# Turning the memory tokens with VectorE's 32x32 block transposes, and the layer norm's tail on pairs of tiles, in a one-core decoder trunk

## What is computed

```python
def rms_norm(x, g):
    xf = x.astype(jnp.float32)
    y = xf * lax.rsqrt(jnp.mean(xf * xf, axis=-1, keepdims=True) + EPS)
    return (y * g.astype(jnp.float32)).astype(x.dtype)

# once, for both layers
mkv = (rms_norm(mem, mem_norm_g) @ w_mem_kv).reshape(bsz, mlen, 2, MEM_HEADS, MEM_HEAD_DIM)
mem_k = rms_norm(mkv[:, :, 0], mem_k_norm_g)
mem_v = mkv[:, :, 1]

# even layer, convolution group: c is the depthwise convolution over 1024 channels
c = layer_norm(c, ln_g, ln_b)
o_b = (jax.nn.silu(c.astype(f32)) * jax.nn.silu(z_b.astype(f32))).astype(h.dtype)
```

## Time and profile before

| | us |
|---|---|
| median of 3 runs (1311.61 to 1311.96) | 1311.9 |
| the profiled execution | 1310.86 |
| its span | 1309.1 |
| TensorE busy | 1303.0 (100%) |
| VectorE busy | 988.7 (76%) |
| ScalarE busy | 749.9 (57%) |
| GpSimd busy | 90.4 (7%) |
| SyncE queue's bytes | 267.00 MB, 67.0% of 16 engines' time |

### The profile page before, as it was taken

The page is one execution under the profiler, slowest core; times in us unless marked ns, Lnnn a source line. Parts: engine busy times, 40 slices in busy tenths (PEclk is TensorE's granted clock), DMA queues, the critical chain, the costliest instruction groups (busy, mean ns, idle before and its releaser), DMA issues.

```text
span 1309.1 us, 17285 instructions
## 1 busy us (share of the span) xinstructions
PE 1303.0 (100%) x6221; PEld 1092.9 (83%) x6221; DVE 988.7 (76%) x1548; ACT 749.9 (57%) x1175; POOL 90.4 (7%) x91
## 2 busy tenths in 40 slices
PE   9999999999999999999999999999999999999998
PEld 9898888888888888888888888888888888888887
DVE  5467588888988898887667487797788788668563
ACT  6556643567435556586346447748657568554341
POOL 2000200102000100100000020020100200000000
PEclk9999999999999999999999999999999999999999
DMA  9675465876775996785768664765765766977662
GB/s 316 203 207 180 151 200 163 221 213 202 213 212 165 299 314 219 220 241 159 215 207 259 195 194 152 248 194 174 228 194 174 227 192 192 284 214 220 199 194 80
DMA packets 182158, 272.82 MB, mean 208 GB/s; under 512 B 42384, under 2 KB 63801, under 8 KB 182073
## 3 DMA queue, kind: packets, MB, share of 16 engines
q1 hardware_dynamic: 179353, 267.00, 67.0%
q10 hardware_dynamic: 2720, 4.72, 1.1%
HBM read 251.10 MB, written 20.58 MB: 208 GB/s over the span
## 4 chain that ended last, share of the span: by engine, by line
PE 98%; DMA 1%; DVE 0%; ACT 0%; issue 0%; SPq 0%; ACTq 0%
PE job L1990 58%; PE job L2000 29%; PE job L1987 2%; PE mixer L2212 1%; PE mixer L2200 1%; PE mixer L2011 1%; PE job L1997 1%; PE mixer L2122 1%; PE mixer L2222 1%; PE mixer L2230 1%; PE mixer L2102 1%; PE mixer L2135 1%; DMA raw<-in_ev_w_in_dram 1%; DVE wlo L1463 0%; PE mixer L2221 0%; PE mixer L2232 0%
## 5 line engine op out<-in xcount | busy, mean ns | idle before, releaser
L1990 PE MATMUL job<-whi,xhi 128*128 128x512 f32 x1660 | 660.6, 398 | 0.0
L1990 PE MATMUL job<-whi,xlo 128*128 128x512 f32 x1660 | 647.1, 390 | 0.0
L1463 DVE TENSOR_TENSOR wlo<-raw,whi 128x1024 fp32r<-128x1024 f32 x431 | 527.3, 1244 | 88.2 <-ACT whi L1094 87.2
L1094 ACT ACTIVATE whi<-raw 128x1024 fp32r<-128x1024 f32 x431 | 445.6, 1056 | 220.6 <-PE job L2000 180.8
L2000 PE MATMUL job<-wlo,xhi 128*128 128x512 f32 x1660 | 444.1, 389 | 0.0
L2000 PEld LDWEIGHTS job<-wlo,xhi 128*128 128x128 f32 x1660 | 311.6, 188 | 65.6
L1990 PEld LDWEIGHTS job<-whi,xhi 128*128 128x128 f32 x1660 | 311.9, 188 | 62.5
L1990 PEld LDWEIGHTS job<-whi,xlo 128*128 128x128 f32 x1660 | 312.0, 188 | 62.2
L1736 DVE SCALAR_TENSOR_TENSOR cvr<-cvr,vt 128x255 f32<-128x255 f32 (+14 forms) x240 | 99.2, 472 | 0.0
L1127 ACT ACTIVATE proj<-job,rstd 128x512 f32<-128x512 f32 x76 | 47.9, 683 | 64.4 <-PE job L2000 43.7
L1496 DVE TENSOR_TENSOR hid<-hid,job 128x512 f32<-128x512 f32 x46 | 29.5, 684 | 39.6 <-PE job L2000 39.6
(11 more groups left out here) (307 smaller groups left out, 957.0 us busy)
## 6 DMA issues: line engine op xcount, KB each, us to landing
raw<-in_od_w_in_dram SPq DMA_DIRECT2D x160, 512.0 KB, 4.1
raw<-in_ev_w_in_dram SPq DMA_DIRECT2D x143, 512.0 KB, 4.5
raw<-in_ev_w_out_dram SPq DMA_DIRECT2D x48, 512.0 KB, 5.3
raw<-in_od_w_out_dram SPq DMA_DIRECT2D x48, 512.0 KB, 5.5
raw<-in_w_mem_kv_dram SPq DMA_DIRECT2D x32, 512.0 KB, 4.9
proj<-turned_blocks SPq DMA_DIRECT2D x68, 128.0 KB, 5.2
turned_blocks<-proj SPq DMA_DIRECT2D x9, 512.0 KB, 4.4
turned_blocks<-mix SPq DMA_DIRECT2D x7, 512.0 KB, 3.7
```

What stands on the lines that cost most here:

```text
L1094: act(whi[:, c % RING, :, :], raw[:, c % RAWS, :, :], ACT.Copy).then_inc(s_hi, 1)
L1463: vec.tensor_tensor(wlo[:, c % RING, :, :], raw[:, c % RAWS, :, :], whi[:, c % RING, :, :].bitcast(F32), ALU.subtract).then_inc(s_lo, 1)
L1990: mm(pj[j % 2][n][:, :], x[:, s, cols], h, start=first, stop=False)
```

## The change

`mem` is loaded in another layout: partition 32b + j of `memx` holds, for a = 0 to 7, columns 512b to 512b + 511 of token 32a + j. A transpose of 32x32 blocks on VectorE (`do_mt`, eight steps of 128x512, two fills each) then gives tiles whose rows are features 512b + 32k + j', in `memt`, tiles 4 to 7 of `mix`. The rows of `w_mem_kv` and of `mem_norm_g` are loaded in the same order: each chunk of the memory jobs by four DMAs of 32 partitions, the gains in runs of 32 elements. ScalarE and VectorE split the fills from `memt`; TensorE's transposes are gone. ScalarE's squares become eight of 512 columns, whose sums stand by (b, j) in `msum`; GpSimd puts them by token into `mquar` in 16 copies, and VectorE adds the four quarters. The layer norm's tail works on pairs of tiles: VectorE multiplies by the token factors alone, and ScalarE applies gain and bias in one instruction per tile. Fills 40 to 47 move one position later, and a tap pair's planned share is 0.29 for 0.31. The last wait of the turn `lt` 7 is now for all 16 memory fills.

```diff
-CONV_SHARE = 0.31
+CONV_SHARE = 0.29
...
-                "d5e": .1, "d6": .25, "gate": .25, "za": .45, "glu": .45, "zg": .65, "lt": .47, "nt": .5, "xt": .18, "mf": .16, "bas": .1}
+                "d5e": .1, "d6": .25, "gate": .25, "za": .45, "glu": .45, "zg": .65, "lt": .47, "nt": .5, "xt": .18, "mt": .26, "mf": .16, "bas": .1}
...
-        stream(5, CH0[J_OB] + k // 2 - 3, [(("mf", F_OB + k), 0)])
+        stream(5, CH0[J_OB] + k // 2 - 2, [(("mf", F_OB + k), 0)])
...
-        stream(5, CH0[J_MEM] - 11 + k, [(("xt", F_MEM + k), 0)])
-        stream(5, CH0[J_MEM] - 2 + k, [(("xt", F_MEM + 8 + k), 0)])
+        for half, start in ((0, CH0[J_MEM] - 11 + k), (8, CH0[J_MEM] - 2 + k)):
+            if k % 2 == 0:
+                stream(5, start - 1, [(("mt", (half + k) // 2), 0)])
+            stream(5, start, [(("xt", F_MEM + half + k), 0)])
...
-    for n in range(10):
-        p = stream(2, p, [(("ln" + "abo"[i], n - i), 0) for i in range(3) if 0 <= n - i < 8] + [("wait", 1)])
+    for n in range(6):
+        p = stream(2, p, [(("ln" + "abo"[i], n - i), 0) for i in range(3) if 0 <= n - i < 4] + [("wait", 1 + n % 2)])
...
-        memx = reg[:, :].rearrange("p (t d) -> p t d", t=T)
+        memx = reg[:, :].rearrange("p (a d) -> p a d", a=8)
+        memt = mflat[:, 4 * S:8 * S].rearrange("p (k s) -> p k s", k=4)
...
+                if name == "mem":
+                    for b in range(4):
+                        src = w[name][:, c0:c0 + 512].rearrange("(b k j) n -> b j k n", b=4, j=32)[b, :, 2 * (c - CH0[j]):2 * (c - CH0[j]) + 2]
+                        sp.dma_start(raw[32 * b:32 * b + 32, c % RAWS, :, :], src).then_inc(s_raw[c % RAWS], 16)
+                    return
...
+            for n, (dst, src) in enumerate(vecs(vrow)[1:]):
+                if n == 0:
+                    src = src.rearrange("k p -> (k p)").rearrange("(b k j) -> k b j", b=4, j=32)
+                    dst = dst.rearrange("k (b j) -> k b j", b=4)
...
             def do_rstd(src):
+                if src == 1:
+                    gp.wait_ge(s_ss, 2)
+                    for a in range(4):
+                        for b in range(4):
+                            ins = nc.gpsimd.tensor_copy(mquar[32 * a:32 * a + 32, :, b], msum[32 * b:32 * b + 32, a:8:4])
+                    ins.then_inc(s_mquar, 1)
...
+                if F_MEM <= n < F_OB:
+                    sc.wait_ge(s_jt, turn_count["mt", (n - F_MEM) // 2])
+                    fill_wait(n)
+                    act(xhi[:, SLOT[n], :], memt[:, n % 4, :], ACT.Copy, scale=xt_gain(n)).then_inc(s_xh, 1)
+                    return
...
+                if src == 1:
+                    for a in range(8):
+                        ins = act(pflat[:, 512 * (a % 4):512 * (a % 4) + 512], memx[:, a, :], ACT.Square, accum_out=msum[:, a:a + 1])
+                        if a == 3:
+                            link(ins)
+                    ins.then_inc(s_ss, 1)
+                    return
...
-            def do_lnb(ct):
-                sc.wait_ge(s_xn, ct + 2)
-                act(cvr[:, ct, :], cvr[:, ct, :], ACT.Identity, bias=gain("ev_ln_b", ct)).then_inc(s_ly, 1)
-                sc.wait_ge(s_ly, ct + 1)
-                if ct >= 2:
-                    sc.wait_ge(s_mixb, ct - 1)
-                act(cvr[:, 8 + ct % 2, :], cvr[:, ct, :], ACT.Tanh, scale=0.5).then_inc(s_lt, 1)
+            def do_lnb(a):
+                sc.wait_ge(s_xn, a + 2)
+                for ct in (2 * a, 2 * a + 1):
+                    ins = act(cvr[:, ct, :], cvr[:, ct, :], ACT.Identity, bias=gain("ev_ln_b", ct), scale=gain("ev_ln_g", ct))
+                link(ins)
+                if a:
+                    sc.wait_ge(s_mixb, 2 * a)
+                act(cvr[:, 8:10, :], cvr[:, 2 * a:2 * a + 2, :], ACT.Tanh, scale=0.5).then_inc(s_lt, 1)
...
-                sc.dma_start(memx[:, :, 512 * b:512 * b + 512],
-                             mem[:, 512 * b:512 * b + 512].rearrange("(t p) d -> p t d", p=128)).then_inc(s_min, 16)
+                sc.dma_start(memx[32 * b:32 * b + 32], mem[:, 512 * b:512 * b + 512].rearrange("(a j) d -> j a d", j=32)
+                             ).then_inc(s_min, 16)
...
+            def do_mt(p):
+                ve.wait_ge(s_min, 64)
+                ve.wait_ge(s_xl, F_OA + 8 if p < 2 else F_MEM + 2 * p - 2)
+                vec.transpose(memt[:, 2 * (p % 2):2 * (p % 2) + 2, :].rearrange("p k s -> p (k s)"),
+                              memx.rearrange("p a (k j) -> p k a j", j=32)[:, 2 * p:2 * p + 2]).then_inc(s_jt, 1)
...
+                if src == 1:
+                    ve.wait_ge(s_mquar, 1)
+                    link(vec.tensor_reduce(ssq[:, src, :], mquar[:, :, :], AX.X, ALU.add))
...
+            def do_lna(a):
                 ve.wait_ge(s_xn, 1)
+                v = cvr[:, 2 * a:2 * a + 2, :]
+                vec.tensor_tensor(v, v, lnacc[:, :].unsqueeze(1).broadcast_to([128, 2, S]), ALU.mult).then_inc(s_xn, 1)
+
+            def do_lno(a):
+                c = cvr[:, 2 * a:2 * a + 2, :]
+                ve.wait_ge(s_lt, a + 1)
+                ve.wait_ge(s_z, 2 * a + 2)
+                link(vec.scalar_tensor_tensor(out=c, in0=cvr[:, 8:10, :], scalar=1.0, in1=c, op0=ALU.add, op1=ALU.mult))
+                v = mix[:, 8 + 2 * a:10 + 2 * a, :]
+                vec.scalar_tensor_tensor(out=v, in0=c, scalar=0.25, in1=v, op0=ALU.mult, op1=ALU.mult).then_inc(s_mixb, 2)
...
-                    ve.wait_ge(*((s_z, 16) if e == 6 else (s_xl, F_OA + 8)))
+                    ve.wait_ge(*((s_z, 16) if e == 6 else (s_xl, F_OB)))
...
             def do_xt(n):
-                if F_H <= n < F_H + 12:
+                if F_MEM <= n < F_H + 12:
                     return
...
-                elif n < F_OB:
-                    src, k = memx, n - F_MEM
-                    pe.wait_ge(s_min, 64)
```

More of the change, by code:

```diff
@@ L403, in prog @@
         qgain = sb("qgain", [128, 1])
+        msum = sb("msum", [128, 8])
+        mquar = sb("mquar", [128, T, 4])
         rows = sb("rows", [128, 2, 128], F32R)
@@ L497, in prog @@
         turn_no = {i: n for n, i in enumerate(i for st, i in plan if st == "lt")}
-        turn_count = {q: n + 1 for n, q in enumerate(q for q in plan if q[0] in ("lt", "nt"))}
+        turn_count = {q: n + 1 for n, q in enumerate(q for q in plan if q[0] in ("lt", "nt", "mt"))}
         def exchanged(e, transfers=5):
@@ L644, in prog @@
         s_xn = sem("ln_reciprocals_then_scaled")
-        s_ly = sem("ln_affine")
+        s_mquar = sem("mem_square_sums_by_token")
         s_lt = sem("ln_tanh")
@@ L699, in banks @@
             if step == "xt":
-                return [] if F_H <= i < F_H + 12 else [i % 3 if 8 <= i < F_OB else i % 4]
+                return [] if F_MEM <= i < F_H + 12 else [i % 3 if 8 <= i < F_OA else i % 4]
             if step == "mao":
@@ L789, in turned @@
         def turned(n):
-            return n + 1 if n < F_OA else n - F_MEM + 17 if n < F_OB else n - F_H - 12 + 33
+            return n + 1 if n < F_OA else n - F_H - 12 + 17
         def mix_tile(n):
@@ L1088, in split @@
                     return
-                sc.wait_ge(s_raw[c % RAWS], 16 * (c // RAWS + 1))
+                sc.wait_ge(s_raw[c % RAWS], 16 * (c // RAWS + 1 + 3 * sum(CH0[J_MEM] <= b < CH0[J_MEM + 4] for b in range(c % RAWS, c + 1, RAWS))))
                 if c >= RING:
@@ L1161, in do_rstd @@
                     sc.wait_ge(s_xl, F_H + 8)
+                if src == 1:
[5 more added lines that the diff above has]
+                    return
                 o = 2048 if src == 0 else 0
-                link(act(pflat[:, 0:2048], (memx if src == 1 else hid)[:, 0, :], ACT.Square, accum_out=ssq[:, src, 0:1]))
-                ins = act(pflat[:, o:o + 2048], (memx if src == 1 else hid)[:, 1, :], ACT.Square, accum_out=ssq[:, src, 1:2])
+                link(act(pflat[:, 0:2048], hid[:, 0, :], ACT.Square, accum_out=ssq[:, src, 0:1]))
+                ins = act(pflat[:, o:o + 2048], hid[:, 1, :], ACT.Square, accum_out=ssq[:, src, 1:2])
                 ins.then_inc(s_ss, 1)
@@ L1352, in squares @@
                 if i == 4:
-                    sc.wait_ge(s_xp, turned(F_MEM + KT - 1))
+                    sc.wait_ge(s_xl, F_OB)
                 unused = reg[:, 3072:4096] if i >= 4 else scr
@@ L1505, in do_first @@
                 ve.wait_ge(s_vt, 1)
+            def do_mt(p):
[3 more added lines that the diff above has]
+                              memx.rearrange("p a (k j) -> p k a j", j=32)[:, 2 * p:2 * p + 2]).then_inc(s_jt, 1)
             def do_xt(n):
                 ve.wait_ge(s_xh, n + 1)
+                if F_MEM <= n < F_OB:
+                    vec.scalar_tensor_tensor(out=xlo[:, SLOT[n], :], in0=memt[:, n % 4, :], scalar=xt_gain(n),
+                                             in1=xhi[:, SLOT[n], :].bitcast(F32), op0=ALU.mult, op1=ALU.subtract).then_inc(s_xl, 1)
+                    return
                 if F_H <= n < F_H + 12:
@@ L1756, in do_lnr @@
```

(6 more changed lines are left out.)

1 line of the change is left out of this document (removed).

## The result

The changed kernel takes **1313.47 us** at the median of 20 runs (1312.44 to 1314.57), the kernel before 1311.46 us at the median of 20 beside it (1311.05 to 1311.96). The ratio is 1.0016, with a 95% interval of 1.001 to 1.0023. It is slightly slower, where 1307.9 us was forecast. Its profiled execution took 1313.76 us, 2.90 more than the profiled execution of before, with a span of 1312.0.

A forecast was written before the change was run, and what follows sets the result against it. TensorE, busy 1303.0 of 1309.1 us, was taken as the bound. Removing 16 transpose pairs at 0.253 us saves 4.05 us, all else hidden: 1311.9 - 4.05 = 1307.9 us, 8-in-10 range 1307.2 to 1310.4.

The forecast's parts named there:

- Layer norm: VectorE's layer norm tail: 24 instructions of 256 become 12 of 512, some 2 us less, off the path; ScalarE about even.
- cost to TensorE nothing: Conv taps packed closer by the smaller share: at worst 3.0 us unplanned VectorE work; thinnest lead 3.4 us, at chunk 108.
- the cover is the lead of the chunk remainders: Chunks 150 to 190: VectorE's remainders at least 8.1 us ahead of TensorE, which was to hide the added work.
- rival 1: VectorE waits for GpSimd's copies, using up the lead; TensorE stands 2 to 4 us; 1310 to 1312 us; 12%.
- VectorE, turns and remainders: Memory stretch: eight turns add 5.6 us, fill remainders from SBUF save 1.0; lead expected to stay near 8 us.
- rival 2: Small losses together: remainders 1.4 to 4 us late around chunks 160 to 175; 1309.5 to 1312 us; 10%.
- Square sums: ScalarE's squares 6.5 us against 4.2; GpSimd's 16 copies 0.15 us each, 2.4 in all; VectorE waits about nothing, at most 9.3.
- The transposes: TensorE's 16 pairs of memory transposes in as many chunk slots: 0.253 us a pair, 4.05 us gained by removing them.
- SyncE: Memory chunk loads as four DMAs: 1.7 us of issue a chunk, under 2.72; any 1.3 us wait covered by the lead.
- rival 3: SyncE's queue becomes the bound in chunks 160 to 191; slower by 0.2% from 0.87 us an issue, up to 1366 us; 4%.
- The conv half's fills: Fills before chunk 192, one slot later: 8.1 us of margin leaves over 3 us, so no cost.
- The sign that I named: A TensorE wait on remainders near chunk 166 would prove the forecast wrong by rival 1.

The follow-up runs named there:

- the pair of 1311.9 and 1307.85: Changed kernel, memory fills 34 to 39 up to three positions earlier, lnm at 172: 1311.9 us; with the last two additions moved to VectorE too: 1307.85 us.
- the version with all four edits: Changed kernel with memory fills earlier, lnm at 172, square sums' factors at 164 and the last two additions on VectorE: 1307.48 us, ratio 0.997.
- the last version: Changed kernel with memory fills earlier, lnm at 172 and the last two additions on VectorE, factors not moved: 1307.85 us (1307.0 to 1311.39).

## Why the prediction was wrong

**The step that failed** is "*Layer norm* ... off the path" together with "cost to TensorE nothing" for the taps, and with them the sentence that the cover is the lead of the chunk remainders. The sum has no term for GpSimd's additions or for where their products stand in the plan. That lead is one margin of several. The first use of the layer norm on TensorE is `lnm`, which had 0.3 us of margin, not 8; and the 3925 ns of the earlier trace rows, which I quoted for rival 1, were the first of the two additions that it waits for. I used that row as a price for copies and did not ask who waited for the additions themselves. Nor did I work out the plan's new positions: the smaller share and the new steps moved `lnm` one chunk forward, 2.72 us, against those 0.3. It measured 2.73 us of wait and 1.8 of lower clock, 4.5 in the profiled execution. Wait and fill stall alone, 2.7 and 1.4 us, eat the gain of 4.05; the clock's 1.8, with the first chunks and chunk 93, make the profiled execution slower. The run of the kernel before with `lnm` at 170 and its twin with two additions on VectorE (1312.83 and 1311.48 us) show this without the change; the pair of 1311.9 and 1307.85 shows it in the changed kernel.

**"VectorE, turns and remainders ... Net 4.6 us in 48 us, hidden by the lead"** failed in its cover, not in its price. A turn took 0.70 us as said; a remainder from SBUF 0.48 and not 0.42, so 5.6 and not 4.6 us were added. For chunk remainders the cover held, though the lead did not stay near 8: its lowest value between chunks 150 and 190 sank from 8.2 to 5.3 us (chunks 156 and 157). A fill's remainder is made only 1.2 chunks before its use, and fill 39 had 3.3 us. TensorE's own gain is what eats such a margin: it arrives up to 4 us earlier at everything that it did not have to wait for before. It cost 1.37 us. This is rival 2 in its place (chunk 167) and its size (1.4 us), for the most part; that rival had 10%.

**"Square sums ... it stands still for about nothing"**: the copies took 246 ns each on the mean (4.55 us for 16, median 182 ns, one 1092), where I took 150, and VectorE waited 1.72 us. ScalarE's eight squares ended 5.1 us after they began, where I had 6.5. Rival 1 in its own form, the lead of the remainders used up, did not come; with the wait moved away the kernel took 0.65 us less, which is not resolved.

**What was right.** The transposes: 0.25 us a pair and 4.05 us in all, to the hundredth. That gain showed at the end only where nothing else was late: 1311.43 - 1307.48 = 3.95 us in the version with all four edits, 0.4 us from the forecast. SyncE: four DMAs for one cost nothing (1311.2 against 1311.22), rival 3 falls; in the changed kernel a piece took 0.427 us to issue at the median and landed in 4.1, where a whole load of the memory had landed in 4.9. (Rival 3's threshold for a time slower by 0.2% was mis-worked: with its own 12 us of lead it is 0.83 us an issue and not 0.87.) The conv half's fills, one slot later, brought no wait. The taps' closer packing costs nothing by itself (1311.32 against 1311.29), but it also moves what stands behind it, which the prediction left out. The advice against a transpose on VectorE did not matter: VectorE was at 75%, TensorE at 99%.

**The sign that I named** as proof against me, a TensorE wait near chunk 166, came at 167. The larger one, at 170, breaks "no wait of TensorE between 470 and 620 us", but it is a wait on GpSimd, which no rival had.

Not settled: the 0.74 us at chunk 93; why the clock fell behind one wait of 2.7 us and not behind another; and the split of the last 3.5 us in the version with only the additions moved, for want of a comparable profile.

## What to carry to other kernels

Where one engine is the bound and you take work off it, it reaches every other dependency earlier by what you took off. List for the stretch behind the edit each first use of something made by another engine, with its margin, and compare the smallest with your gain; the lead of the main stream says nothing about side products. When a planner places the steps, work out the new positions of all of them: a changed share moves steps that the diff does not mention.

Small work for GpSimd should not be due just when VectorE can run ahead with two-input instructions. A row far above its group's median (3925 ns against 852) is the place to ask who waits for it.

## What was unexpected of the hardware

Two additions of 128x256 on GpSimd took 2.42 us in one version and 3.35, 3.64, 4.77, 5.92 and 7.04 in others, longer where more of VectorE's two-input remainders ran back to back beside them: 3.64 us beside two, 4.77 beside three, 5.92 beside four, 7.04 beside five, 1.13 us more for each, which is the distance from one remainder's start to the next. In each of these executions the pair ended 1.4 to 1.5 us behind the last remainder (542.11 against 540.67 in the changed kernel, 545.33 against 543.89 beside five), no more than two such additions take undisturbed (0.72 to 0.75 us each). So GpSimd got hardly anything done until the train was over. The Trainium skill, "SBUF — State Buffer", "SBUF: two separate sides", has a VectorE instruction with two SBUF inputs and a GpSimd instruction exclude each other for a whole instruction on the port pair that they share; the rows agree, and they show that GpSimd can lose up to five turns in a row.

A wait of TensorE can cost more than its length, and how much more isn't told by the length. Behind 2.73 us of idleness the granted clock was 0.60 for 3 us, 1.8 us more; behind 2.1 us, in the version that took 1311.9 us, it fell to 0.50 and also cost 1.8; behind 3.14 us it was 0.50 for 4 us and cost 3.2. Behind 2.74 us, in the version with the factors later, it stayed at 1.00 and cost 0.3. The wait of 1.1 us of the kernel before with `lnm` at 170 also cost 0.3 beyond its length. That would also make executions of one version scatter: most versions with such a wait do by 2 to 7 us (the kernel before with `lnm` at 170, where no clock was lost, by 1.3), most without by 0.5 to 2.2, and the last version, with 4.4, is the exception. As one execution of each was profiled, this is argued and not shown.
